# Hybrid decoder layer on one core: modulation vectors summed in pairs, attention values in a PSUM bank of their own, a moved router bias, and one expert load behind the first gather

## The reference

```
mod = silu(c) @ ada_w + ada_b                  # six vectors of 1024
sh_a, sc_a, gt_a, sh_f, sc_f, gt_f = split(mod, 6)
h    = rmsnorm(x, g) * (1 + sc_a) + sh_a
proj = h @ w_in                                # gated linear attention (GLA) and window attention
mix  = concat(gla(...), window_attention(...)) @ w_out
x    = x + gt_a * mix
h    = rmsnorm(x, g2) * (1 + sc_f) + sh_f
logits = h @ w_router + b_router               # 4 groups and 32 experts
y    = sum over 2 chosen experts of weight * (silu(h @ w_gate) * (h @ w_up)) @ w_down
out  = rmsnorm(x + gt_f * y, g3)
```

## Time and profile before

| | us |
|---|---|
| three executions | 631.59, 625.77, 630.77 |
| median | 630.77 |
| profiled execution, its time | 629.8 |
| profiled execution, span of the trace | 628.0 |
| PE busy | 507.3 (81% of the span) |
| DVE, ACT, POOL busy | 272.3, 146.8, 80.3 |

### The profile page before, as it was taken

One profiled execution on the slowest core, in us unless ns is written; L12 is line 12 of the kernel. 1 busy time (PEld: TensorE's weight loads), 2 busy tenths in 40 slices (PEclk: granted clock), 3 DMA queues, 4 the chain that ended last, 5 costly groups with the idle time before them and its releaser, 6 DMA issues.

```text
span 628.0 us, 6963 instructions
## 1 busy us (share of the span) xinstructions
PE 507.3 (81%) x2628; PEld 295.0 (47%) x2628; DVE 272.3 (43%) x653; ACT 146.8 (23%) x371; POOL 80.3 (13%) x128
## 2 busy tenths in 40 slices
PE   0497999998979898999972999998777796888900
PEld 0453675545546555455561555554444453444400
DVE  4679728475437374454651152322222021222246
ACT  3402123323414171211121121211111021111111
POOL 5000000000000000001213112221111121121101
PEclk9999899999959998999975999998999798989965
DMA  8997937807200005730039599999999999999374
GB/s 296 380 360 232 369 141 273 294 36 214 54 0 2 2 0 201 307 128 35 33 109 362 196 419 416 416 414 417 412 416 416 416 419 416 414 417 386 128 288 154
DMA packets 51099, 163.10 MB, mean 260 GB/s; under 512 B 10301, under 2 KB 11342, under 8 KB 42618
## 3 DMA queue, kind: packets, MB, share of 16 engines
q1 hardware_dynamic: 40632, 151.10, 62.0%
q0 software_dynamic: 5312, 8.48, 3.7%
q10 hardware_dynamic: 5122, 3.08, 1.6%
HBM read 158.63 MB, written 12.91 MB: 273 GB/s over the span
## 4 chain that ended last, share of the span: by engine, by line
PE 58%; DMA 21%; SPq 8%; DVE 6%; issue 3%; ACT 2%; ACTq 1%; POOL 0%; POOLq 0%; DVEq 0%
PE ps L1385 18%; DMA ring<-in_w_up 16%; PE ps L1647 10%; PE ps L1569 9%; PE ps L1661 4%; SPq L459 3%; SPq L463 2%; SPq L460 2%; DMA xres<-in_x 2%; PE ps L1501 1%; DMA proj<-h_rows,hreg 1%; PE ps L1433 1%; PE ps L1595 1%; PE ps L1474 1%; PE ps L1641 1%
## 5 line engine op out<-in xcount | busy, mean ns | idle before, releaser
L1385 PE MATMUL ps<-ring,hreg 128*128 128x512 f32 (+1 forms) x320 | 132.0, 568 | 2.1 <-DVE hreg L982 2.1
L1647 PE MATMUL ps<-ring,proj 128*64 128x256 f32 x336 | 87.0, 418 | 20.4 <-DMA ring<-in_w_up 18.8
L1385 PEld LDWEIGHTS ps<-ring,hreg 128*128 128x128 f32 x320 | 61.4, 196 | 62.6 <-issue 57.4
L1648 PE MATMUL ps<-ring,proj 128*64 128x256 f32 x336 | 87.1, 418 | 0.0
L1302 DVE TENSOR_TENSOR proj<-proj,ps 64x256 f32<-64x256 f32 x33 | 13.9, 422 | 162.4 <-ACT proj L883 162.4
L1647 PEld LDWEIGHTS ps<-ring,proj 128*64 128x64 f32 x336 | 48.8, 150 | 48.1 <-DMA ring<-in_w_up 16.3
L953 DVE SCALAR_TENSOR_TENSOR wide<-wide,csil 128x512 f32<-128x512 f32 x72 | 49.1, 746 | 2.0 <-DMA wide<-in_ada_w 2.0
L883 ACT ACTIVATE proj<-ps 64x256 f32<-64x256 f32 x33 | 12.4, 377 | 156.4 <-PE ps L1648 156.4
L639 POOL DMA_INDIRECT y_rows<-proj,hreg x33 | 32.9, 997 | 124.0 <-DVE proj L1308 124.0
L1648 PEld LDWEIGHTS ps<-ring,proj 128*64 128x64 f32 x336 | 48.8, 150 | 0.0
L588 POOL TENSOR_TENSOR rstd<-ssq,halfm 128x1 f32<-128x1 f32 (+1 forms) x13 | 9.9, 765 | 239.6 <-DVE ssq L1250 157.7
(11 more groups left out here) (278 smaller groups left out, 712.0 us busy)
## 6 DMA issues: line engine op xcount, KB each, us to landing
wide<-in_ada_w SPq DMA_DIRECT2D x24, 1024.0 KB, 8.6
ring<-in_w_gate SPq DMA_DIRECT2D x21, 1024.0 KB, 19.8
ring<-in_w_up SPq DMA_DIRECT2D x21, 1024.0 KB, 22.6
ring<-in_w_down SPq DMA_DIRECT2D x21, 1024.0 KB, 23.1
wide<-in_w_down SPq DMA_DIRECT2D x12, 1024.0 KB, 23.9
ring<-in_w_in SPq DMA_DIRECT2D x4, 2048.0 KB, 9.9
wide<-in_w_gate SPq DMA_DIRECT2D x6, 1024.0 KB, 21.1
wide<-in_w_up SPq DMA_DIRECT2D x6, 1024.0 KB, 24.7
```

What stands on the lines that cost most here:

```text
L1385: mm = pe.matmul(ps[bank_of(st)][:, 0:CW[ch]], hT[:, k, b * P:(b + 1) * P], win_sb[ch][:, k, :], start=k == 0, stop=k == KD - 1)
L1647: pe.matmul(ps[bank][0:TILE, 0:F], hx[:, k, :], wg_sb[w][:, k, :], start=k == 0, stop=k == KD - 1)
L1648: mm = pe.matmul(ps[bank][TILE:P, 0:F], hx[:, k, :], wu_sb[w][:, k, :], start=k == 0, stop=k == KD - 1)
```

## The change

- The pieces of `sc_f` and of `sh_f` are summed two at a time: eight products with 128 weight columns over both halves of `acc` replace twice eight with 64 columns. The entries `("mod", 6)` and `("mod", 8)` go.
- `attn_value` writes PSUM bank 6 and no longer waits for ACT's copies of the next block's queries and keys.
- `bias_sum` moves from behind round 0 to just ahead of the first output projection, and the sum over the partitions becomes an entry `bias` of its own behind it, in bank 4, which DVE reads directly; ACT's copy goes. Entries that share memory with it get waits.
- `places` on PE becomes `count`; DVE's `places` stand later than before: for block 2 behind `x_turn` of block 3, and PE's `ids` of block 2 behind the router product of block 3.
- SP loads expert 4 when the first gather has landed, and no longer straight behind expert 3.
- The gate and up products of the first expert of a gathered pair wait for the transposed pieces one by one, in the order 0, 4, 1, 5, 2, 6, 3, 7, and not for all eight.

```diff
-     ("proj", 0, 3), ("mod", 5), ("ada_sum", 7), ("proj", 1, 0), ("low_turn",), ("mod", 6), ("proj", 1, 1),
+     ("proj", 0, 3), ("mod", 5), ("ada_sum", 7), ("proj", 1, 0), ("low_turn",), ("proj", 1, 1),
...
-    _projected(0, ("proj", 3, 0), ("proj", 3, 1), [("mod", 11)]) + [("bias_sum",)] +
-    _projected(1, ("proj", 3, 2), ("proj", 3, 3), [("mod", NPC)]) +
+    _projected(0, ("proj", 3, 0), ("proj", 3, 1), [("mod", 11)]) + _projected(1, ("proj", 3, 2), ("proj", 3, 3)) +
...
-    [("out_proj", 0, 0, 8), ("mix_turn", 1), ("out_proj", 0, 1, 8), ("gate_scale", 2), ("norm2", 0), ("gate_scale", 3),
+    [("bias_sum",), ("out_proj", 0, 0, 8), ("bias",), ("mix_turn", 1), ("out_proj", 0, 1, 8), ("gate_scale", 2),
+     ("norm2", 0), ("gate_scale", 3),
...
-     ("router", 2), ("out_proj", 3, 1, 8), ("norm2", 3), ("places", 2), ("x_turn", 3), ("rows", 3),
-     ("ids", 2), ("router", 3), ("places", 3), ("ids", 3)]
+     ("router", 2), ("out_proj", 3, 1, 8), ("norm2", 3), ("count", 2), ("x_turn", 3), ("places", 2), ("rows", 3),
+     ("router", 3), ("ids", 2), ("count", 3), ("places", 3), ("ids", 3)]
...
             gates(3, 3)
             downs(3, 3)
-            sp.wait_ge(xn_ready, NB)
-            for b in range(NB):
-                sp.wait_ge(h_stored[b], 16)
+            sp.wait_ge(gath0, 16)
             gates(4, 4)
             downs(4, 4)
...
                if i >= 6:
-                    dve.wait_ge(turn_ready, TURN[("mod", i - 2)] + 1)
+                    last = i - 2 if PARTS[(i - 2) // 2] not in (3, 4) else (i - 2) // 2 * 2 + 1
+                    dve.wait_ge(turn_ready, TURN[("mod", last)] + 1)
...
+                elif kind == "bias":
+                    dve.wait_ge(bias_summed, 1)
+                    dve.tensor_tensor(br[:, :], br[:, :], ps[4][:, 0:NR], ALU.add).then_inc(bias_out, 1)
...
                         for k in range(KD):
-                            mm = pe.matmul(bank[(i % 2) * TILE:(i % 2 + 1) * TILE, k:k + 1],
-                                           acc[:, i % 2, :].rearrange("p (q k) -> p k q", k=KD)[:, k, :],
+                            mm = pe.matmul(bank[:, k:k + 1],
+                                           acc.rearrange("p a n -> p (a n)").rearrange("p (q k) -> p k q", k=KD)[:, k, :],
...
                     pe.wait_ge(probs_copied, 4 * (n + 1))
-                    if n + 1 < NB:
-                        pe.wait_ge(attn_copied, 5 * (n + 2))
...
-                            mm = pe.matmul(ps[3][kv * HD:(kv + 1) * HD, :],
+                            mm = pe.matmul(ps[6][kv * HD:(kv + 1) * HD, :],
...
+                elif kind == "bias":
+                    pe.wait_ge(bias_ready, 1)
+                    pe.wait_ge(attn_out, NB)
+                    pe.matmul(ps[4][:, 0:NR], ones[:, :], wsum, start=True, stop=True).then_inc(bias_summed, 1)
...
-            def gate_up(bank, w, hx, done):
+            def gate_up(bank, w, hx, done, copies=0):
 
-                for k in range(KD):
+                for k in [0, 4, 1, 5, 2, 6, 3, 7]:
+                    if copies:
+                        pe.wait_ge(e_tokens_act if k >= 4 else e_tokens_dve, copies + k % 4)
```

More of the change, by code:

```diff
@@ L97 @@
      ("out_proj", 1, 0, 4), ("x_turn", 0), ("out_proj", 1, 0, 8), ("rows", 0), ("mix_turn", 2), ("out_proj", 1, 1, 4),
      ("router", 0), ("out_proj", 1, 1, 8), ("norm2", 1),
-     ("out_proj", 2, 0, 4), ("places", 0), ("x_turn", 1), ("out_proj", 2, 0, 8), ("rows", 1), ("ids", 0),
+     ("out_proj", 2, 0, 4), ("count", 0), ("places", 0), ("x_turn", 1), ("out_proj", 2, 0, 8), ("rows", 1), ("ids", 0),
      ("mix_turn", 3), ("out_proj", 2, 1, 4), ("router", 1), ("out_proj", 2, 1, 8), ("norm2", 2),
-     ("out_proj", 3, 0, 4), ("places", 1), ("x_turn", 2), ("out_proj", 3, 0, 8), ("rows", 2), ("ids", 1),
@@ L102 @@
-     ("router", 2), ("out_proj", 3, 1, 8), ("norm2", 3), ("places", 2), ("x_turn", 3), ("rows", 3),
-     ("ids", 2), ("router", 3), ("places", 3), ("ids", 3)]
+     ("out_proj", 3, 0, 4), ("count", 1), ("places", 1), ("x_turn", 2), ("out_proj", 3, 0, 8), ("rows", 2), ("ids", 1),
+     ("router", 2), ("out_proj", 3, 1, 8), ("norm2", 3), ("count", 2), ("x_turn", 3), ("places", 2), ("rows", 3),
+     ("router", 3), ("ids", 2), ("count", 3), ("places", 3), ("ids", 3)]
 )
@@ L268, in layer_kernel @@
             sem(n) for n in ('x1_turned', 'x1_copied', 'bias_ready', 'bias_out'))
[L269 to L270 removed]
+        ids_ops, ids_summed, bias_summed = (
+            sem(n) for n in ('ids_ops', 'ids_summed', 'bias_summed'))
         logits_ready, logits_read, pairs_marked, places_ready = (
@@ L754, in _ @@
                         rows = slice((i % 2) * TILE, (i % 2 + 1) * TILE)
-                        if i == NPC:
-                            act.activation(bsum, bank[:, 0:NR], ACT.Copy).then_inc(turn_free, 1)
-                        elif PARTS[i // 2] == 2:
+                        if PARTS[i // 2] == 2:
                             act.activation(gt_a[:, half], bank[:, :], ACT.Copy).then_inc(turn_free, 1)
@@ L761, in _ @@
                         else:
-                            act.activation(fcol[rows, 4 - PARTS[i // 2], :], bank[rows, 0:KD], ACT.Copy)\
+                            act.activation(fcol[:, 4 - PARTS[i // 2], :], bank[:, 0:KD], ACT.Copy)\
                                 .then_inc(turn_free, 1)
@@ L843, in _ @@
                         continue
+                    if b == 0 and i == 0:
+                        act.wait_ge(bias_summed, 1)
                     cols = slice(512 * i, 512 * (i + 1))
@@ L1426, in _ @@
                     pe.wait_ge(turn_free, r - 1)
[L1427 to L1430, removed]
+                    if PARTS[i // 2] in (3, 4):
                         pe.wait_ge(acc_ready, i + 1)
                         for k in range(KD):
-                            mm = pe.matmul(bank[(i % 2) * TILE:(i % 2 + 1) * TILE, k:k + 1],
-                                           acc[:, i % 2, :].rearrange("p (q k) -> p k q", k=KD)[:, k, :],
+                            mm = pe.matmul(bank[:, k:k + 1],
+                                           acc.rearrange("p a n -> p (a n)").rearrange("p (q k) -> p k q", k=KD)[:, k, :],
                                            ones[:, 0:1], start=True, stop=True)
@@ L1613, in _ @@
                     mm.then_inc(gla_out, 1)
-                elif kind == "places":
+                elif kind == "count":
                     b = st[1]
```

16 lines of the change are left out of this document (6 added, 10 removed).

## The result

| | us |
|---|---|
| changed kernel, median of 4 runs (lowest, highest) | 604.94 (602.42, 612.33) |
| before, median of 4 runs | 628.34 (625.77, 631.59) |
| ratio, 95% interval | 0.961 (0.953 to 0.969) |
| forecast | 606.3 (602.0 to 614.0) |
| profiled execution after: span | 601.6 (before 628.0) |

The account below looks back on a forecast made before the run. It took PE to bound the mixer and output projection, and the weight stream the experts. Mixer 19.1 us plus router, gather and first product 5.4 gave 24.5 us less: 606.3 us, range 602.0 to 614.0 (own range 602.5 to 609.5).

Parts of the forecast that it names:

- Pair sums: In PE's mixer chain, two of four 2.01 us sums go and the merged groups stay at 2.01 us: gain 4.0 us.
- Values in their own bank: In the mixer rounds, PE's wait on ACT's copies goes: 1.8 us each in rounds 0 and 2, together 3.6 us.
- The bias in round 1: From projection end to GLA output, round 1 takes 7.7 us instead of 19.36, PE keeping its clock: 11.7 us less.
- The moved DVE steps: The three bias_sum steps, about 1.5 us, just fit DVE's 1.65 us idle time ahead of the first residual.
- Router of block 3: PE's router product starts right after ACT's copy, no longer behind DVE's places and copy: 0.8 us earlier.
- First gather: With expert 4 held back, the gather issued at 330.4 lands at 335.2, not 339.56: 4.3 us earlier, router's 0.8 included.
- First release of a slot: First expert product waits for one copy, not four (1.1 us); the release moves from 349.42 to 344.0, the stream following.
- the lower clock in round 1: Rival: the clock falls in round 1 nonetheless, or elsewhere at the same price, 6.7 us: 613.0 us; chance 0.17.
- the slow gather: Rival: the first gather is slow by itself, landing at 338.8, gaining 1.9 us instead of 5.4: 609.8 us; chance 0.12.
- the slow stage of the output projection: Rival: the clock stays at its lower level through the output projection, costing 55 us: 661 us; chance 0.03.
- The first rival's other half: The clock falls not in round 1 but in another place at the same price, 6.7 us; chance 0.17 for both halves.
- The doubled load of the pair sums: Rival: loading twice the columns takes twice as long, a group 4.0 us, so no gain: 610.3 us; chance 0.06.

Follow-up runs that it names:

- e4: Changed kernel, but DVE's last addition of pieces 6 to 9 writes its sums in the order PE loads them: 604.07 us, ratio 0.960.
- c1: The kernel before, unchanged, profiled a second time: 634.67 us, one execution.
- c2: The kernel before, unchanged, profiled a third time: 629.84 us, one execution.
- e2: The kernel before with only the bank edit (values in bank 6, without their wait): 619.02 us, ratio 0.984.
- e5: Changed kernel with expert 4's load back straight behind expert 3's: 611.03 us, ratio 0.972.
- e6: Changed kernel with the loads of experts 3 and 4 both behind the first gather: 613.95 us, ratio 0.979.
- e7: Changed kernel, but a pair's first expert waits for all eight transposed pieces, in the new order: 607.39 us, ratio 0.970.
- c3: The changed kernel again, unchanged, as a control and for a second profile: 611.23 us, ratio 0.967.
- e1: The kernel before with the bias edit alone: 620.95 us, ratio 0.987.

## Why the prediction was right, point by point

- **Pair sums: wrong in size.** The step "leave the group at 2.01 us: gain 4.0" failed. The group took 3.58 us and the gain was 0.9 us. I had taken the price from the transposes' strided load, 193 ns; the products' strided load of 128 columns took 335 ns. The Trainium skill's rule ("TensorE: Matmul & The Clock Gate", "LDWEIGHTS (loading the stationary operand)": the time goes with the columns) was the better guide for this pair, 217 ns to 335, though it would have doubled the time. But e4 has 128 columns in 192 ns. At 128 columns the stride costs 143 ns, and the rule does not speak of it. Why a transpose loads the same stride in 193 ns stays open; the traces show only that a product of these sums stands there as two instructions and a transpose as one. The profile still shows 2.5 us at the operands of round 0. The remainder is the fall between 75.2 and 78.6 us in the kernel before, behind its first group. The prediction had no term for falls behind the groups, before or after.
- **Values in their own bank: right.** 1.9 us in round 0 and 1.9 in round 2, 1.8 forecast. The query product was not late.
- **The bias in round 1: right in size, too narrow in cause.** From round 0's output to round 1's it is 26.2 us against 38.1, 11.9 less, 11.7 forecast. c1 and c2 show that the long fall stands in every profile that has both idle times, and e2 that it can stay away with the 2.9 us alone. The sum was right because the change removes both; what each of them does is not shown.
- **The moved DVE steps fit**, as the 1.65 us of the earlier trace rows said. DVE's timeline in the changed kernel, the last bias step and the first residual:

```profile
236.35 0.45 DVE L1037 TENSOR_TENSOR wr<-wr,fcol 128x288 f32<-128x288 f32 x1
237.02 0.69 DVE L1169 TENSOR_TENSOR early<-ps,early 128x512 f32<-128x512 f32 x1 [0.22 <-PE ps L1562]
```

  0.22 us are left of the 1.65.
- **Router of block 3: right.** The product starts behind ACT's copy, 1.81 us after the block's transposes and not 2.68: 0.9 us, 0.8 forecast.

```profile
298.77 0.60 ACT L850 ACTIVATE hreg<-ps 128x512 f32<-128x512 f32 x1 [0.51 <-PE ps L1575]
...
299.42 2.23 PE L1588 MATMUL ps<-wr,hreg 128*128 128x36 f32 x16 [0.69 <-ACT hreg L850]
```

- **First gather: right.** 5.1 us from issue to landing, 4.8 forecast (330.4 to 335.2), and e5 and e6 bear out the mechanism on both sides.
- **First release of a slot.** SP's timeline: expert 3, expert 4, and expert 5's first and last load:

```profile
303.20 0.33 SPq L458 DMA_DIRECT2D wide<-in_w_gate  x1
...
315.39 0.33 SPq L458 DMA_DIRECT2D hreg<-in_w_gate  x1
...
323.45 0.33 SPq L458 DMA_DIRECT2D ring<-in_w_gate  x1
...
331.28 0.38 SPq L462 DMA_DIRECT2D ring<-in_w_down  x1
```

  7.9 us from the first transposes to the release, against 9.7. 1.0 us of this is the waiting piece by piece (e7); the remainder is an earlier rise of the clock in this profile (8.5 us in c3). The stream follows with nothing lost: from expert 5's down weights to the end 270.3 us, 270.8 before. The margin, 0.8 us by the estimate, was enough, and e6 shows the cost beyond it.
- **Not foreseen:** 1.6 us in round 3, where the clock stayed at 1.00 behind the idle 2.75 us in the first profile of the changed kernel. It fell there in the three profiles of the kernel before, and in c3.
- **The range.** The forecast's own 602.5 to 609.5 us doesn't follow from the parts named for it: added up, they give 599.4 to 610.3.

So the total of the first profile, 26.4 us, is 24.5 with 3.1 us too much for the pair sums, and 5 us more that came from the clock (1.6 in round 3, 0.7 in the first product, about 1.6 behind 75 us) and from tenths in the other steps. That the two nearly cancel is luck, and so is part of the near hit in the median. The medians of the changed kernel were 604.9 us in the first four runs and 611.2 us in the six of c3, which is 23.4 and 19.0 us under the kernel before beside them; the forecast of 24.5 us lies above both.

The rivals: the lower clock in round 1, the slow gather and the slow stage of the output projection were not seen. The first rival's other half, a lower clock in another place at the same price, was: c3 has it behind both groups and is 6.4 us late at the output projection. That is also one of the prediction's own signs of being wrong (0.50 where the profile before has 1.00), which the first profile doesn't show and c3 does. The doubled load of the pair sums was nearly right as a mechanism (3.58 us a group, 4.0 in the rival); I had given it 0.06.

## What to carry to other kernels

A short wait on the engine that sets the time can cost several times its length when it brings the clock down: read the granted clock of the stretch behind it, and compare with the same work in another round. Where two idle times stand close to each other, removing either may do, as e1 and e2 show. Profile the same kernel more than once before you call a fall of the clock a property of the code, and note what stands just ahead of each fall. An operand that the matrix engine loads should be written in the order of the load: here one strided write on an engine with time to spare more than halved the group. And a transfer that much work waits for should go ahead of those that nobody needs yet, but hold back only as many of these as fit into the time in which the transfers would stand still.

## What the runs showed of the hardware that I had not expected

- Weight load of 128 float32 columns for a product: 192 ns with neighbouring elements, 335 ns with every eighth (e4 and the changed kernel); 217 ns for 64 columns at the same stride.
- The clock falls to its lower level (1.2 of 2.4 GHz), for 3 to 7 us, also where PE has no gap, in places that differ between executions of the same kernel: from 83.9 and from 118.0 us in c3, neither in the first profile. All eighteen such falls between 55 and 130 us begin 2 to 5 us after the start of a group of sixteen one-column products with a weight load each. With c3's fall behind an idle time of 3.9 us at 60 us they make it 5.3 us late at the operands of round 0. Why a group does it in one execution and not in another stays open.
- An idle time of 2.9 us in round 1 did not bring the clock down in the one profile of e2; in the three of the kernel before the clock fell in it or at its end. 2.75 us in round 3 did in ten profiles of twelve.
- A gather of 0.5 MB: 3.4 us with no weights ahead of it, 5.1 us behind 3.1 MB, 8.3 us behind 6.3 MB.
